# Two self-attention loops with a third probability buffer, another order on each engine, and evenly spread projection pieces

## The chip, the cores and the metric

The kernel runs on one core of a Trainium2 chip. The metric is device time in microseconds, the median of three runs. A core has TensorE (matmuls, with a separate queue of weight loads), VectorE, ScalarE, GpSimd, and SyncE, which here issues most of the transfers. Each engine executes its own instructions in order, and engines wait for each other through semaphores.

## What is computed

Two transformer blocks on 512 tokens of width 1024, in float32. The first block (dilated attention, convolutional feed-forward) isn't touched. The second block computes three attentions from one projection, gates and merges them, and then runs a mixture of 16 experts. Cut to the two attentions concerned:

```
h = rmsnorm(x);  proj = h @ w_in
# differential attention: 8 heads, two maps m each, head size 64, value size 128
sc = q[m] . k[m] * scale - slope[head] * |qpos - kpos|      # 512 x 512
p  = softmax(sc);  a = p[0] - lam * p[1];  o = a @ v
# window attention: 16 heads of 64, 4 key heads, window of 128 to each side
sc = q . k * scale - slope[head] * dist, or -inf outside the window
p  = softmax(concat(sc, sink))[:-1];  o = p @ v
```

## The kernel before

The sequence has 4 query blocks of 128 rows. The first changed loop, here DA, is differential attention: 16 units u (and two more rounds to drain), a unit being one head (u // 2) and half of the query blocks (u % 2), so four score tiles of 128 x 512 (two query blocks, two maps). The second, WA, is window attention: 16 units of one pair of heads and two query blocks, four score tiles of 128 x 256 or 128 x 384. All is written out by hand, engine by engine; the order in each queue is the order of the code.

One round u of DA, before:
- TensorE: four score matmuls of unit u into four PSUM banks (L1507); the product with V of unit u-2 (L1516); eight transposes of the probabilities of unit u-1 (L1526); then the fill of this round.
- VectorE: the probabilities of unit u-1 (`da_probs`: reciprocal L1049, L1051, then for each of two query blocks a scaling L1054 and a multiply-add L1055); then for unit u four times "add the distances, write to `da_e`, take the maximum" (L1071) and the negated maximum (L1076).
- ScalarE: the PSUM eviction of a finished fill job (L697, L701); the output of a head (L710); two copies of transposed probabilities of u-1 (L717); four exponentials of u, in place, with row sums (L722).
- GpSimd: it splits the projection weights of the fill into a high and a low part (L457, L460), two instructions for each job of 128 output features, as soon as the buffers of the job two before are free; between these it makes the distance tables of later heads (L505; for WA L509, in pairs), released by the maxima that last used them.

`da_e`, `da_pt`, `mx`, `nmx`, `lsum` have two copies each, used by u % 2. Because of that the maxima of unit u wait until the transposes of u-2 have been done.

Round u of WA is alike: scores (L1542), product with V of u-2 (L1558), then eight transposes of u-1 in two groups (L1567), two k of fill, a third group of two transposes, which needs the PSUM bank that ScalarE has emptied by its first copy, then the rest of the fill. ScalarE copies all three groups (L742) and then does the exponentials of u (L755, and L757 for the sink). VectorE does probabilities of u-1 (L1085, L1086, L1090), then maxima (L1105, L1110) of u.

The fill (`FILL1`, `FILL2`, `proj_part`) is the projection of later inputs: 10 jobs of 8 k in DA and 8 jobs of 8 k in WA, where one k is three matmuls of 128 x 512 (L1486 to L1488; high x high, high x low, low x high). All jobs use PSUM bank 3, so each waits for ScalarE's eviction of the one before. In DA the even jobs lie whole in round 3c, the odd ones in two halves in rounds 3c+1 and 3c+2; in WA each job has four k in each of two rounds.

Of the kernel before, what the change touches and what calls it, by code (L numbers as in the profile page):

```python
# [15 lines left out]
S, D, P = 512, 1024, 128  # L16
TT, KT = S // P, D // P
# [28 lines left out]
def build(nc, I, out):  # L46
# [3 lines left out]
    with ctx:  # L50
# [99 lines left out]
        da_e = ar(4096, 2, 4, S)  # L150
        da_pt = ar(8192, 2, 4, 256)
        wdist = ar(11776, 384)
        dist = ar(12160, 896)
        alibi = ar(13056, 2, 896)
        walibi = ar(13312, 4, 384)
        lamv = ar(8192, 4, 64)
        wa_q, wa_k, wa_v = ar(0, KT, S), ar(27136, WA_KV, S), ar(29184, TT, 256)
        o_wa = wa_q
        wa_p = ar(4096, 2, 4, 384)
        wa_pt = ar(8192, 20, P)  # L160
        memt = ar(23040, 2, D)
        memn = ar(25088, 2, D)
        junkm = ar(12160, D)
# [92 lines left out]
        FILL1 = [[] for _ in range(18)]  # L256
        FILL2 = [[] for _ in range(18)]
        for j in range(10):
            if j % 2 == 0:
                FILL1[3 * (j // 2)] = [(j, range(8))]  # L260
            else:
                FILL1[3 * (j // 2) + 1] = [(j, range(4))]
                FILL1[3 * (j // 2) + 2] = [(j, range(4, 8))]
        for j in range(8):
            FILL2[2 * j] = [(j, range(4))]
            FILL2[2 * j + 1] = [(j, range(4, 8))]

        def fill_ended(fill, u):

            return [j for j, ks in fill[u] if ks[-1] == KT - 1] if u >= 0 else []  # L270
# [161 lines left out]
        def _(pool):  # L432
# [85 lines left out]
            wtmp = ar(30208, 384)  # L518
# [45 lines left out]
        def _(act):  # L564
# [139 lines left out]
            for u in range(18):  # L704
                for j in fill_ended(FILL1, u - 1):
                    wa_feature(j)
                if u >= 3 and u % 2:
                    h = (u - 3) // 2
                    act.wait_ge(dpv, u - 1)
                    A(o_raw[:, h, :], ps[:, 2, :], F.Copy).then_inc(dO_ev, 1)  # L710
# [8 lines left out]
                if u < 16:  # L719
                    act.wait_ge(dnm_done, u + 1)  # L720
                    for i in range(4):
                        last = A(da_e[:, u % 2, i, :], da_e[:, u % 2, i, :], F.Exp, bias=nmx[:, u % 2, i:i + 1],  # L722
                                 accum_out=lsum[:, u % 2, i:i + 1])
                    last.then_inc(de_done, 1)
            act.dma_start(memt, I["mem_2"][0].rearrange("(t p) d -> p t d", p=P)).then_inc(in_mem, 16)

            act.wait_ge(in_small, 96)
            for u in range(18):
                for j in fill_ended(FILL2, u - 1):
                    act.wait_ge(pj_ps, J_F2 + j + 1)  # L730
                    A(xa_q[:, j, :], ps[:, 3, :], F.Copy, scale=0.0625).then_inc(pjA, 1)
                if u >= 3 and u % 2:
                    act.wait_ge(wpv, u - 1)
                    A(o_wa[:, (u - 3) // 2, :], ps[:, 2, :], F.Copy).then_inc(wO_ev, 1)
                if 1 <= u <= 16:
                    m = u - 1
                    for i, nb in enumerate((4, 4, 2)):
                        act.wait_ge(wt_ps, 3 * m + i + 1)
                        if m >= 2:
                            act.wait_ge(wpv, m - 1)  # L740
                        b0 = 10 * (m % 2) + 4 * i
                        A(wa_pt[:, b0:b0 + nb, :], ps[:, i % 2, 0:nb * P].rearrange("p (b q) -> p b q", b=nb),  # L742
                          F.Copy).then_inc(wpt_done, 1)
# [5 lines left out]
                if u < 16:  # L749
                    act.wait_ge(wnm_done, u + 1)  # L750
                    p, qh = u // 2, u % 2
                    for i in range(4):
                        c0, c1 = (P if (qh, i // 2) == (0, 0) else 0), (256 if (qh, i // 2) == (1, 1) else 384)
                        v = wa_p[:, u % 2, i, c0:c1]
# [5 lines left out]
                    last.then_inc(we_done, 1)  # L760

# [93 lines left out]
        def _(dve):  # L855
# [190 lines left out]
            def da_probs(u):  # L1046
# [5 lines left out]
                for i in range(2):  # L1052
                    e0, e1 = da_e[:, u % 2, 2 * i, :], da_e[:, u % 2, 2 * i + 1, :]
# [5 lines left out]
            for u in range(17):  # L1059
                if u:  # L1060
                    da_probs(u - 1)
                if u < 16:
# [3 lines left out]
                    if u >= 2:  # L1066
                        dve.wait_ge(dt_ps, 2 * (u - 1))
                    for i in range(4):
                        qb = 2 * (u % 2) + i // 2
                        dve.wait_ge(sd_ps, 4 * u + i + 1)  # L1070
                        V.tensor_tensor_reduce(out=da_e[:, u % 2, i, :], in0=ps[:, 4 + i, :],  # L1071
# [21 lines left out]
            for u in range(17):  # L1093
                if u:
                    wa_probs(u - 1)
# [690 lines left out]
```

## Time and profile before

| | |
|---|---|
| median of three runs | 2738.1 us (2730.5 to 2738.1) |
| profiled execution | 2739.4 us, span 2737.6 us |
| TensorE matmul busy | 2386.6 us (87%) |
| VectorE, ScalarE, GpSimd busy | 948.2, 497.2, 1024.2 us |
| mean granted TensorE clock | 0.959 of full speed |

The trace times are counted from the span's start. TensorE's matmuls are pipelined, so two of them overlap in the rows; the time of a sequence is read from start to start. "Idle before" is the idle time of the engine ahead of an instruction, with what ended it. A granted clock of 1 is 2.4 GHz, one of 0.5 is 1.2 GHz, and a value between them is a mean over time.

### The profile page before, as it was taken

To read this page: it belongs to the slowest core of one execution; us is meant where nothing else is said; L and a number is where in the kernel's file an instruction comes from. 1 tells how busy PE (TensorE), PEld (TensorE's weight loads), DVE (VectorE), ACT (ScalarE), POOL (GpSimd) and SP (SyncE) were. 2 spreads that over 40 slices of the span, in tenths; PEclk is the share of its full clock that TensorE was granted. 3 is DMA by queue.
4 is the path that set the end of the run, shared out by engine and by line. 5 is a ranking of instruction groups with operands and counts; after the bars stand their busy time and mean duration, and the time that the engine had idled before them with its cause. 6 is when DMAs were issued, how large, how long until landed. Compare 5 with 4: busy or idle time off the path is not lost.

```text
span 2737.6 us, 27015 instructions
## 1 busy us (share of the span) xinstructions
PE 2386.6 (87%) x11244; PEld 1581.4 (58%) x11244; DVE 948.2 (35%) x1323; ACT 497.2 (18%) x1067; POOL 1024.2 (37%) x497
## 2 busy tenths in 40 slices
PE   6999968999989988787899999599888888888886
PEld 4778837887878856565668887533323232332322
DVE  4664664555020156544732363401111101021012
ACT  2324222121010044454431010100000000000001
POOL 5444606888787744332538887200000000000000
PEclk9999989999999999898999999699999999999999
DMA  4211202322222210100213224489999999999996
GB/s 133 70 47 47 93 0 66 104 93 92 93 93 79 93 47 31 47 32 31 93 53 101 93 93 154 184 363 416 416 418 417 418 417 417 416 416 417 417 418 279
DMA packets 172341, 527.43 MB, mean 193 GB/s; under 512 B 9954, under 2 KB 92091, under 8 KB 139451
## 3 DMA queue, kind: packets, MB, share of 16 engines
q1 hardware_dynamic: 169008, 521.17, 49.1%
q10 hardware_dynamic: 3211, 4.51, 0.5%
q8 instruction: 90, 1.47, 0.2%
q14 instruction: 32, 0.26, 0.0%
HBM read 523.56 MB, written 2.10 MB: 192 GB/s over the span
## 4 chain that ended last, share of the span: by engine, by line
PE 67%; DMA 13%; DVE 12%; ACT 5%; issue 2%; ACTq 0%; POOL 0%; SPq 0%; DVEq 0%; POOLq 0%
PE ps L1298 9%; PE ps L1299 9%; PE ps L1300 9%; PE ps L1756 8%; PE ps L1729 7%; DMA hT<-in_w_exp_up 5%; PE ps L1451 4%; DMA arena<-in_w_exp_up 4%; DMA ring<-in_w_exp_up 4%; PE ps L1314 3%; PE ps L1315 2%; PE ps L1316 2%; PE ps L1690 2%; ACT arena L722 1%; PE ps L1714 1%
## 5 line engine op out<-in xcount | busy, mean ns | idle before, releaser
L457 POOL TENSOR_TENSOR w_hi<-ring,one 128x1024 fp32r<-128x1024 f32 x208 | 403.8, 1942 | 516.4 <-PE ps L1300 285.7
L460 POOL TENSOR_TENSOR w_lo<-ring,w_hi 128x1024 fp32r<-128x1024 f32 x222 | 543.4, 2448 | 58.0 <-ACT w_hi L773 41.6
L1298 PE MATMUL ps<-h_hi,w_hi 128*128 128x512 f32 x864 | 346.2, 401 | 8.4 <-DVE h_lo L880 5.8
L1300 PE MATMUL ps<-h_hi,w_lo 128*128 128x512 f32 x864 | 337.7, 391 | 0.0
L1299 PE MATMUL ps<-h_lo,w_hi 128*128 128x512 f32 x864 | 337.7, 391 | 0.0
L552 POOL TENSOR_TENSOR arena<-arena 128x512 f32<-128x512 f32 x8 | 8.4, 1048 | 834.6 <-PE ps L1702 796.8
L1729 PE MATMUL ps<-ring,arena 128*64 128x512 f32 x944 | 212.6, 595 | 42.6 <-DMA ring<-in_w_exp_up 41.8
L1729 PE MATMUL ps<-arena 128*64 128x512 f32 x848 | 191.9, 595 | 39.8 <-DMA arena<-in_w_exp_up 39.8
L1298 PEld LDWEIGHTS ps<-h_hi,w_hi 128*128 128x128 f32 x864 | 163.1, 189 | 50.4 <-DVE h_lo L880 6.7
L1299 PEld LDWEIGHTS ps<-h_lo,w_hi 128*128 128x128 f32 x864 | 163.2, 189 | 36.8 <-issue 4.3
L1300 PEld LDWEIGHTS ps<-h_hi,w_lo 128*128 128x128 f32 x864 | 162.9, 189 | 34.6
L1729 PEld LDWEIGHTS ps<-ring,arena 128*64 128x64 f32 x944 | 71.5, 137 | 180.5 <-issue 179.4
L1729 PEld LDWEIGHTS ps<-arena 128*64 128x64 f32 x848 | 64.6, 137 | 164.2 <-issue 164.0
L1234 DVE TENSOR_TENSOR arena<-ps,arena 64x1024 f32<-64x1024 f32 x32 | 39.3, 1227 | 306.1 <-ACT arena L834 305.4
L834 ACT ACTIVATE arena<-ps 64x1024 f32<-64x1024 f32 x32 | 30.8, 1009 | 571.0 <-PE ps L1729 571.0
L1756 PE MATMUL ps<-arena 128*64 128x512 f32 x528 | 123.4, 615 | 11.7 <-DVE arena L1265 11.7
L1243 DVE TENSOR_TENSOR x<-ps,x 128x512 f32<-128x512 f32 x64 | 42.9, 689 | 260.3 <-PE ps L1714 259.9
L908 DVE RECIPROCAL arena<-arena 128x512 f32<-128x512 f32 x24 | 80.5, 3353 | 68.9 <-ACT arena L629 68.8
L1009 DVE SCALAR_TENSOR_TENSOR arena<-ps,vec,arena 128x511 f32<-128x511 f32 (+1 forms) x88 | 59.9, 743 | 110.9 <-ACT arena L668 110.9
L1756 PE MATMUL ps<-ring,arena 128*64 128x512 f32 x416 | 92.2, 593 | 5.5 <-DVE arena L1265 5.5
L1272 DVE COPY arena<-ps 64x512 f32<-64x512 f32 x16 | 11.1, 694 | 225.5 <-PE ps L1756 225.5
L1756 PEld LDWEIGHTS ps<-arena 128*64 128x64 f32 x528 | 38.0, 141 | 87.1 <-issue 72.7
(297 smaller groups left out, 3903.4 us busy)
## 6 DMA issues: line engine op xcount, KB each, us to landing
arena<-in_w_exp_down SPq DMA_DIRECT2D x66, 1024.0 KB, 19.9
ring<-in_w_exp_gate SPq DMA_DIRECT2D x59, 1024.0 KB, 24.1
ring<-in_w_exp_up SPq DMA_DIRECT2D x59, 1024.0 KB, 25.4
arena<-in_w_exp_gate SPq DMA_DIRECT2D x53, 1024.0 KB, 21.8
arena<-in_w_exp_up SPq DMA_DIRECT2D x53, 1024.0 KB, 23.0
ring<-in_w_exp_down SPq DMA_DIRECT2D x52, 1024.0 KB, 22.0
ring<-in_w_in SPq DMA_DIRECT2D x34, 1024.0 KB, 5.1
ring<-in_ffn_w_up SPq DMA_DIRECT2D x22, 1024.0 KB, 5.1
```

Of the source, the lines that this page charges most:

```text
L457: nc.gpsimd.tensor_tensor(hi, w, one[:].unsqueeze(2).to_broadcast(list(w.shape)), ALU.mult).then_inc(w_high, 1)
L460: nc.gpsimd.tensor_tensor(lo, w, hi.bitcast(f32), ALU.subtract).then_inc(w_split, 1)
L908: V.reciprocal(rr[:, n % 2, :], rt[:, n % 2, :]).then_inc(rr_done, 1)
L1009: V.scalar_tensor_tensor(out=v, in0=ps[:, 2 * (j % 2) + i, 0:S - sh], scalar=vec[:, CW + 44 * k + 22 * i + j:CW + 44 * k + 22 * i + j + 1] ...
L1298: mm(o, w[0][:, k, :], h[0][:, k, 0:ntok], start=(k == 0), stop=False)
L1299: mm(o, w[0][:, k, :], h[1][:, k, 0:ntok], start=False, stop=False)
L1300: last = mm(o, w[1][:, k, :], h[0][:, k, 0:ntok], start=False, stop=(k == KT - 1))
L1314: mm(o, hi, w[0][:, k - k0, :], start=(k == 0), stop=False)
L1315: mm(o, hi, w[1][:, k - k0, :], start=False, stop=False)
L1451: last = mm(ps[:, 2 * t + half, :], tile_of(a_, f, t), w_[:, 0, half * 512:half * 512 + 512], start=(f == 0 and a_ is act_hi and w_ is w[0 ...
L1729: last = mm(ps[64 * i:64 * i + 64, c, :], xeT[:, k, a * CAP:(a + 1) * CAP], w[:, c * 512:c * 512 + 512], start=(k == 0), stop=(k == KT - 1))
L1756: last = mm(ps[64 * half:64 * half + 64, 4, :], act_e[:, f, :], w[:, j * D + half * 512:j * D + half * 512 + 512], start=(f == 0), stop=(f ...
```

## The change

- `da_e` and `wa_p` get a third copy (u % 3). `da_pt`, `wa_pt`, the distance tables and scratch areas move to other places of the arena.
- VectorE does the maxima of unit u before the probabilities of u-1, in both loops. The maxima wait for the transposes of u-3 instead of u-2; the negated maximum waits also for the exponentials of u-2.
- ScalarE does the exponentials of u before the head's output and the copies of u-1. In WA the third copy of u-2 comes ahead of the exponentials of u, the first two copies of u-1 behind them.
- TensorE: each round's fill has two parts, one ahead of the product with V, one behind it and ahead of the transposes, which are last in the round. In DA two jobs are spread over three rounds as 3+3, 2+3, 2+3 k; in WA each round has 2+2. In WA the third group of transposes moves to the next round, right behind its scores.
- ScalarE evicts a job that ended in a second part at the start of the next round, one that ended in a first part in the same round ahead of the exponentials.

```diff
-        da_e = ar(4096, 2, 4, S)
-        da_pt = ar(8192, 2, 4, 256)
+        da_e = ar(4096, 3, 4, S)
+        da_pt = ar(10240, 2, 4, 256)
...
-        wa_p = ar(4096, 2, 4, 384)
-        wa_pt = ar(8192, 20, P)
+        wa_p = ar(4096, 3, 4, 384)
+        wa_pt = ar(8704, 20, P)
...
+        for c in range(5):
+            j = 2 * c
+            FILL1[3 * c] = ((j, range(3)), (j, range(3, 6)))
+            FILL1[3 * c + 1] = ((j, range(6, 8)), (j + 1, range(3)))
+            FILL1[3 * c + 2] = ((j + 1, range(3, 5)), (j + 1, range(5, 8)))
         for j in range(8):
-            FILL2[2 * j] = [(j, range(4))]
-            FILL2[2 * j + 1] = [(j, range(4, 8))]
+            FILL2[2 * j] = ((j, range(2)), (j, range(2, 4)))
+            FILL2[2 * j + 1] = ((j, range(4, 6)), (j, range(6, 8)))
...
             for u in range(18):
-                for j in fill_ended(FILL1, u - 1):
+                for j in fill_ended(FILL1, u - 1, 1) + fill_ended(FILL1, u, 0):
                     wa_feature(j)
+                if u < 16:
+                    act.wait_ge(dnm_done, u + 1)
+                    for i in range(4):
+                        last = A(da_e[:, u % 3, i, :], da_e[:, u % 3, i, :], F.Exp, bias=nmx[:, u % 2, i:i + 1],
+                                 accum_out=lsum[:, u % 2, i:i + 1])
+                    last.then_inc(de_done, 1)
                 if u >= 3 and u % 2:
...
             for u in range(17):
-                if u:
-                    da_probs(u - 1)
                 if u < 16:
...
-                    if u >= 2:
-                        dve.wait_ge(dt_ps, 2 * (u - 1))
+                    if u >= 3:
+                        dve.wait_ge(dt_ps, 2 * (u - 2))
...
+                    if u >= 2:
+                        dve.wait_ge(de_done, u - 1)
                     V.tensor_scalar(nmx[:, u % 2, :], mx[:, u % 2, :], -1.0, None, ALU.mult).then_inc(dnm_done, 1)
+                if u:
+                    da_probs(u - 1)
...
+                if FILL1[u][0]:
+                    proj_part(J_F1 + FILL1[u][0][0], FILL1[u][0][1])
                 if u >= 2:
...
                     last.then_inc(dpv, 1)
+                if FILL1[u][1]:
+                    proj_part(J_F1 + FILL1[u][1][0], FILL1[u][1][1])
                 if 1 <= u <= 16:
...
+                if u >= 2:
+                    pe.wait_ge(wpt_done, 3 * (u - 2) + 1)
+                    wa_T(u - 2, 2)
+                if FILL2[u][0]:
+                    proj_part(J_F2 + FILL2[u][0][0], FILL2[u][0][1])
...
-                if 1 <= u <= 16:
-                    pe.wait_ge(wpt_done, 3 * m + 1)
-                    wa_T(m, 2)
-                for j, ks in FILL2[u]:
-                    proj_part(J_F2 + j, ks[2:])
```

## Rows read from the trace of the kernel before

**Rows 1.** Windows: us, busy (count) of PE, PEld, DVE, ACT, POOL; clock; DMA; GB/s.

```profile
965.70:1142.00 176.30, 143.22 (x628) 99.64 (x630) 113.74 (x243) 79.18 (x186) 71.14 (x37) 0.91 0.11 36
1142.00:1299.00 157.00, 122.65 (x800) 92.52 (x796) 72.42 (x240) 75.40 (x228) 47.86 (x28) 0.87 0.11 34
```

**Rows 2.** Chain of waits, 960 to 1300, shares by line.

```profile
by line: ACT arena L722 10.8%; ACT arena L755 10.2%; issue 9.8%; PE ps L1567 8.3%; DVE arena L1071 7.3%; DVE arena L1054 7.2%; DVE arena L1090 5.6%; PE ps L1486 4.5%; DVE arena L1055 4.5%; PE ps L1487 4.4%; PE ps L1488 4.3%; PE ps L1516 2.8
```

**Rows 3.** Waits, 965 to 1130: us in total, times, longest.

```profile
DVE rl L1049 <- ACT arena L722: 49.4, 16, 3.7
...
PE ps L1526 <- DVE arena L1055: 22.8, 9, 5.1
```

**Rows 4.** Waits, 1130 to 1295, same columns.

```profile
DVE lsum L1085 <- ACT esink L757: 76.8, 16, 7.2
...
PE ps L1567 <- DVE arena L1090: 33.7, 16, 4.3
```

**Rows 5.** Timeline of VectorE, one DA unit: start, us, engine, line, operation, [idle before].

```profile
1062.75 0.68 DVE L1071 CUSTOM_DVE_ANT_0 arena<-ps,arena 128x512 f32<-128x512 f32 x1
...
1065.31 0.17 DVE L1076 TENSOR_SCALAR nmx<-mx 128x4 f32<-128x4 f32 x1
...
1068.48 0.18 DVE L1049 RECIPROCAL rl<-lsum 128x4 f32<-128x4 f32 x1 [3.00 <-ACT arena L722]
...
1070.67 0.75 DVE L1055 SCALAR_TENSOR_TENSOR arena<-arena,rl 128x512 f32<-128x512 f32 x1
```

**Rows 6.** Timeline of all engines, 1000 to 1022: GpSimd and VectorE.

```profile
1003.02 2.45 POOL L505 TENSOR_SCALAR arena<-arena 128x896 f32<-128x896 f32 x1 [4.79 <-DVE mx L1071]
...
1007.27 2.38 POOL L457 TENSOR_TENSOR w_hi<-ring,one 128x1024 fp32r<-128x1024 f32 x1 [1.79 <-PE ps L1488]
...
1007.81 2.12 DVE L1054 TENSOR_SCALAR arena<-arena,rl 128x512 f32<-128x512 f32 x1
...
1009.97 2.71 DVE L1055 SCALAR_TENSOR_TENSOR arena<-arena,rl 128x512 f32<-128x512 f32 x1
```

**Rows 7.** Timeline of all engines, 1186 to 1209 (WA).

```profile
1186.93 1.09 PE L1567 MATMUL ps<-ident,arena 128*128 128x128 f32 x8 [0.41 <-DVE arena L1090]
...
1193.35 3.22 DVE L1090 TENSOR_SCALAR arena<-arena,rl 128x384 f32<-128x384 f32 x4
...
1201.25 0.50 ACT L755 ACTIVATE arena<-arena,nmx 128x256 f32<-128x256 f32 x1
...
1202.26 1.35 PE L1542 MATMUL ps<-arena 64*128 64x384 f32 x8
...
1203.54 1.31 PE L1558 MATMUL ps<-arena 128*64 128x128 f32 x20
...
1203.93 0.16 DVE L1085 TENSOR_TENSOR lsum<-lsum,esink 128x4 f32<-128x4 f32 x1 [5.53 <-ACT esink L757]
...
1205.67 1.09 PE L1567 MATMUL ps<-ident,arena 128*128 128x128 f32 x8 [0.82 <-DVE arena L1090]
...
1208.00 0.38 PE L1567 MATMUL ps<-ident,arena 128*128 128x128 f32 x2
```

**Rows 8.** Timeline of all engines, 1000 to 1022: TensorE.

```profile
1001.95 0.40 PE L1488 MATMUL ps<-h_hi,w_lo 128*128 128x512 f32 x1
...
1006.73 0.39 PE L1488 MATMUL ps<-h_hi,w_lo 128*128 128x512 f32 x1
...
1007.05 1.99 PE L1507 MATMUL ps<-arena 64*128 64x512 f32 x8
...
1008.96 1.99 PE L1516 MATMUL ps<-arena 128*128 128x256 f32 x8
...
1012.74 1.09 PE L1526 MATMUL ps<-ident,arena 128*128 128x128 f32 x8 [1.78 <-DVE arena L1055]
```

**Rows 9.** Timeline of TensorE at the end of DA.

```profile
1134.88 1.97 PE L1526 MATMUL ps<-ident,arena 128*128 128x128 f32 x8 [8.80 <-DVE arena L1055]
```

**Rows 10.** Instructions of L1071 over the span: ns min/median/max, first and last start.

```profile
L1071 DVE CUSTOM_DVE_ANT_0 arena<-ps,arena x64: 677/685/692, 969.7 to 1123.9; 128x512 f32<-128x512 f32 x64
```

More of the change, by code:

```diff
@@ L254, in pj_bank_free, with fill_ended @@
                 eng.wait_ge(pjA if PJ[m] == "A" else pjD, PJ[:m + 1].count(PJ[m]))
[L256 to L263, printed above, removed]
-        for j in range(8):
-            FILL2[2 * j] = [(j, range(4))]
-            FILL2[2 * j + 1] = [(j, range(4, 8))]
-        def fill_ended(fill, u):
-            return [j for j, ks in fill[u] if ks[-1] == KT - 1] if u >= 0 else []
+        FILL1 = [((), ()) for _ in range(18)]
+        FILL2 = [((), ()) for _ in range(18)]
+        for c in range(5):
[3 more added lines that the diff above has]
+            FILL1[3 * c + 2] = ((j + 1, range(3, 5)), (j + 1, range(5, 8)))
+        for j in range(8):
+            FILL2[2 * j] = ((j, range(2)), (j, range(2, 4)))
+            FILL2[2 * j + 1] = ((j, range(4, 6)), (j, range(6, 8)))
+        def fill_ended(fill, u, part):
+            job = fill[u][part] if u >= 0 else ()
+            return [job[0]] if job and job[1][-1] == KT - 1 else []
         def pj_all_done(eng, n):
@@ L760, in _ @@
                     last.then_inc(we_done, 1)
+                if u >= 3 and u % 2:
+                    act.wait_ge(wpv, u - 1)
+                    A(o_wa[:, (u - 3) // 2, :], ps[:, 2, :], F.Copy).then_inc(wO_ev, 1)
+                if 1 <= u <= 16:
+                    wa_copy(u - 1, 0)
+                    wa_copy(u - 1, 1)
             act.wait_ge(n_sq, nbase[3] + 2)
@@ L1093, in _ @@
             for u in range(17):
-                if u:
-                    wa_probs(u - 1)
                 if u < 16:
@@ L1113, in _ @@
                                            op0=ALU.mult, op1=ALU.min).then_inc(wnm_done, 1)
+                if u:
+                    wa_probs(u - 1)
             norm(3, memt, memn)
@@ L1525, in _ @@
                         for kb in range(4):
-                            last = nc.tensor.transpose(ps[:, i, kb * P:(kb + 1) * P], da_e[:, m % 2, 2 * i, kb * P:(kb + 1) * P], ident[:])
+                            last = nc.tensor.transpose(ps[:, i, kb * P:(kb + 1) * P], da_e[:, m % 3, 2 * i, kb * P:(kb + 1) * P], ident[:])
                         last.then_inc(dt_ps, 1)
-                for j, ks in FILL1[u]:
-                    proj_part(J_F1 + j, ks)
             pe.wait_ge(sd_done, 64)
@@ L1543, in _, with wa_T @@
                            start=True, stop=True).then_inc(sw_ps, 1)
+                def wa_T(m, i):
+                    for j, (b, qb, kb) in enumerate(WA_UNIT[m % 2][4 * i:4 * i + 4]):
+                        c = (kb - qb + 1) * P
+                        last = nc.tensor.transpose(ps[:, i % 2, j * P:(j + 1) * P], wa_p[:, m % 3, b, c:c + P], ident[:])
+                    last.then_inc(wt_ps, 1)
+                if u >= 2:
+                    pe.wait_ge(wpt_done, 3 * (u - 2) + 1)
+                    wa_T(u - 2, 2)
+                if FILL2[u][0]:
+                    proj_part(J_F2 + FILL2[u][0][0], FILL2[u][0][1])
                 if u >= 2:
@@ L1561, in _ @@
                     last.then_inc(wpv, 1)
-                def wa_T(m, i):
-                    for j, (b, qb, kb) in enumerate(WA_UNIT[m % 2][4 * i:4 * i + 4]):
-                        c = (kb - qb + 1) * P
-                        last = nc.tensor.transpose(ps[:, i % 2, j * P:(j + 1) * P], wa_p[:, m % 2, b, c:c + P], ident[:])
-                    last.then_inc(wt_ps, 1)
+                if FILL2[u][1]:
+                    proj_part(J_F2 + FILL2[u][1][0], FILL2[u][1][1])
                 m = u - 1
```

57 lines of the change are left out of this document (24 added, 33 removed).

## Prediction

> **What bounds the kernel now.** After the page I took the busy time of the two stretches that the change touches. The first loop (differential attention, "DA") fills 965.7 to 1142, 176.3 us; TensorE is busy 143.2 of them, at a mean granted clock of 0.91. The second (window attention, "WA") fills 1142 to 1299, 157.0 us; TensorE is busy 122.7, at 0.87. VectorE is busy 114 and 72 us, ScalarE 79 and 75 [rows 1]. So no engine is full, and TensorE falls now and then from 2.4 to 1.2 GHz.
>
> The chain of waits over both loops says why: it runs over the exponentials (L722, L755), the VectorE lines (L1071, L1054, L1090, L1055) and the transposes (L1567), and the fill matmuls (L1486 to L1488) have only about 4.5% each [rows 2]. The waits agree. In DA VectorE waits 49.4 us for the exponentials (16 times), and TensorE idles 22.8 us ahead of the transposes until L1055 is done [rows 3]. In WA it is 76.8 us (16 times) and 33.7 us [rows 4].
>
> One unit without disturbance shows the ring. In DA: scores added and maximum taken 1062.75 to 1065.31 (2.56), then the exponentials until the reciprocal at 1068.48 (3.17), then the probabilities until 1070.67 + 0.67 (2.86). Sum 8.6 us [rows 5]; 16 units are 137 us. The next unit's maxima come after the probabilities, in the same VectorE queue, and its exponentials after the maxima, so VectorE and ScalarE take turns. The other 39 us are head, tail and collisions: at 1007.81 a scaling takes 2.12 us, and at 1009.97 a multiply-add 2.71; undisturbed these are 0.75 us for the multiply-add and about 0.5 for the scaling (1068.48 to 1070.67 is 2.19 for the reciprocal and L1051, some 0.2 each, two scalings and one multiply-add), each while GpSimd works [rows 5, 6]. In WA the ring is longer: transposes at 1186.93 and 1205.67 are two units apart, 9.4 us each [rows 7], 150 us in 16 units. There ScalarE's third copy, which waits for transposes behind two pieces of fill (1208.00, 2.33 us after the first), lies ahead of the exponentials in ScalarE's queue.
>
> **What the change makes of the ring.** VectorE does maxima(u) before probabilities(u-1), ScalarE does exponentials(u) before the copies of u-1, and the third buffer lets maxima(u) be written while the transposes of u-1 have not read theirs. So exponentials(u-1) run beside maxima(u), and the 3.17 us (DA) and 2.7 us (WA, 1201.25 to 1203.93) [rows 5, 7] leave the ring. Nothing is computed more or less; no DMA moves except the memory load at the end of ScalarE's first loop, which still comes after it. The wait for the exponentials of u-2 ahead of the negated maximum costs nothing: they are a whole unit old. What is late next is TensorE's own queue.
>
> **DA, TensorE work.** Scores 1007.05 to 1008.96: 1.91. The product with V is as long by its row (1.99 with the last one's end, 1.91 by the spacing), transposes 1.09. One k of fill is three matmuls; seven k from 1001.95 to 1006.73 are 0.683 each, 80 k are 54.6 us [rows 8]. 16 x (1.91 + 1.91 + 1.09) + 54.6 = 133.2 us at full clock. One unit with five k is 8.3, with six 9.0.
>
> **DA, where TensorE waits.** Take the time from a unit's first score matmul. Maxima end at 3.2, the negation at 3.4, probabilities at 3.4 + 2.9 = 6.3. The transposes stand in TensorE's queue behind scores, V product and fill, at 7.2 (five k) or 7.9 (six). So an undisturbed unit has 0.9 to 1.6 us of slack, and VectorE is hidden. Disturbed ones are not, and the new order puts the disturbances on the probabilities:
> - A fill job that ends in the first part of a unit (3c+1: units 4, 7, 10, 13) ends at 1.91 + 1.37 = 3.3. That releases GpSimd's two splits, 1.9 and 2.4 us (1007.27 and after: the first began right as its job ended) [rows 6, 8]. The two together cost the probabilities (2.12 - 0.5) + (2.71 - 0.75) = 3.6 us there, so I take 3.7: ready at 10.0, 2.8 late. 4 x 2.8 = 11.2.
> - A slope (2.45 us, released by the last maximum of an odd unit: 1003.02, where now it runs beside the exponentials) [rows 6] falls on the probabilities of units 3, 5, 9, 11: some 2.0 each, ready at 8.4, late by 0.6, 1.2, 0.6 and, with the mask instructions behind it, about 2.7. Sum 5.1. In the other odd units the splits delay the slope past the probabilities.
> - Jobs that end in a second part release splits at about 7.2, and these are over by 3.3 of the next unit. Nothing.
> - Head: VectorE starts 4 us late as now, probabilities(0) meet splits: 4.9. Tail: units 15 to 17 have no fill, and four WA slopes and a split meet the last two probabilities. Now the transposes wait 8.80 us there and run at half clock, 1.97 instead of 1.09 [rows 9, 8]. I take 6.5 for unit 14's, three waits of 0.8 for copies, and 3 for the clock: 11.9.
> - Clock dips elsewhere after a stall: 2.
> Sum: 133.2 + 11.2 + 5.1 + 4.9 + 11.9 + 2 = 168.3, against 176.3: **8 us less**. The bounds: if no collision delays TensorE in the middle and the tail costs half, 133 + 5 + 6 + 2 = 146. If all of GpSimd's 71.1 us in this stretch [rows 1] fell on the ring of scores, maxima, negation, probabilities, transposes (0.6 + 2.6 + 0.2 + 2.9 + 1.1 = 7.4 a unit), 16 x 7.4 + 71 = 189. I stay at 168, since the release times put about half of the splits and slopes there.
>
> The Trainium skill (SBUF — State Buffer, Who interferes with whom) says that VectorE instructions in a two-port mode, or with two SBUF inputs against a GpSimd instruction that reads SBUF, share one port pair with GpSimd under an exclusive lock, and that whoever issues first blocks the other for the whole instruction. That speaks against this order, which places the port-using probabilities right where slopes and splits are released; the durations of 2.12 and 2.71 us agree. The maxima, which read PSUM and SBUF, never grow: 0.677 to 0.692 us in all 64 [rows 10]. By the rule alone and every time lost to it, the result is the third rival below.
>
> **WA, TensorE work.** Scores 1202.26 to 1203.54: 1.28 to 1.35 (1.3), V product 1.3, eight transposes 1.09, two more 0.38 (1208.00) [rows 7], four k of fill 2.73 [rows 8]. 6.85 a unit, 109.6 in all. **Where it waits.** Maxima and negation end at 2.5, probabilities take about 1.8 (VectorE starts at 1203.93 and releases the transposes at 1205.67) [rows 7], ready at 4.3. The transposes are due at 1.35 + 0.38 + 1.37 + 1.3 + 1.37 = 5.8: slack 1.5. Exponentials(u) run 2.6 to 5.3, and the copies of u-1 start at 6.4, so ScalarE (75.4 / 16 = 4.7 of 6.85 us) [rows 1] is hidden too; the third copy now needs transposes that stand right behind the scores, 1.7, before the exponentials can start at 2.6. Jobs end in odd units at 5.8, so their splits are over by 3.2 of the next, even, unit: no cost. Slopes come in pairs, 2.4 us from 2.2 in odd units: ready at about 6.1, 0.4 late, 6 to 8 times, 3 us. In the trace of before a pair of splits makes 3.22 us of the four scalings, about 1.9 too much [rows 7], and that delay I no longer see on the path. Head 2, tail 2.7 (copies that nothing covers), clock 3: TensorE would be 95% busy where it is now 78%, so most of the dips (0.87 mean is 41 us at half clock, 2 x 0.13 x 157) should go. Sum 109.6 + 3 + 2 + 2.7 + 3 = 120.3 against 157.0: **37 us less**. Bounds: 115 with no collision and no dip; with all 47.9 us of GpSimd [rows 1] on a ring of 0.4 + 2.1 + 1.8 + 1.1 + 0.3 = 5.7 a unit, 139.
>
> **After the loops** nothing changes: the memory projection, the gates and the experts start from TensorE's and ScalarE's progress, and SyncE's first expert transfers wait for the gates, so all of it moves earlier by the same amount. The moved buffers (masks, distances, copies) cost nothing by themselves.
>
> **The number.** The profiled execution took 2739.4 us (span 2737.6), 1.3 over the median of the runs, 2738.1. 8.0 + 36.7 = 44.7 less: 2694.7 from the one, 2693.4 from the other. I say 2694.
>
> **Rivals.**
> 1. TensorE-bound: collisions fall beside slack. 146 + 115 = 261 against 333, 72 less: 2666. For it: all slack above is positive without collisions, and the clock rises. Against: the release times of splits in units 4, 7, 10, 13.
> 2. Collisions cost VectorE more than reckoned: halfway between my sum and the upper bounds (189 + 139 = 328): 308, 25 less, 2713. For it: the nine double or single hits could be fourteen. Against: WA's splits lie clear of the probabilities.
> 3. VectorE replaces the ring: every GpSimd instruction hits, 328 us, 5 less, 2733. Within 0.3%. Against: splits released at 7.2 fall on maxima, which don't grow.
> 4. Slower: as 3, and TensorE, waiting 2 to 3 us in each of the 32 units, stays at 1.2 GHz for the scores, copies' wait and V product that follow. Transposes behind a long wait take 0.9 us more [rows 9]; with the V product (1.9 more) 1 to 3 us a unit. With 2 it is 64 us: 328 + 64 - 333 = 59 more, 2797; slower by over 0.3% from 0.4 us a unit on. Against: now waits of 22.8 us in nine leave the mean clock at 0.91 [rows 1, 3].
> 5. It doesn't do what it says: an engine's new order waits for itself, e.g. ScalarE's fill copy ahead of exponentials(u) waits for a job that ends at 3.3, when the maxima are ready at 3.4. Priced 0.5 us in 5 units: nothing against the rest.
>
> **How the numbers follow.** About 0.3% (8 us) can be told from no change. Forecast (2680 to 2706): 0.60. Rival 1 (2660 to 2680): 0.18. Rival 2 (2706 to 2730): 0.15. Rival 3, same: 0.04. Rival 4: 0.03. Range 2664 to 2718. Faster 0.93, same 0.04, slower 0.03.
>
> **What would show it.** In the profile after: VectorE's wait for the exponentials falls from 49 and 77 us to below 10 each; TensorE above 90% busy in WA, with a clock over 0.95, and unit spacing of 6.9 us; in DA spacing of 8.3 to 9 with stretches of 11 in every third unit, where L1054 and L1055 take over 2 us beside L457 and L460. Wrong it would be if the transposes wait in most units of WA, if the slopes' collisions show in even units too, or if a later stage gives the time back by waiting for weights.

## The result, and the profile after

The changed kernel takes 2685.7 us in the median (2681.1 to 2690.9, four runs) against 2734.9 for the kernel before; the ratio is 0.982 [0.980, 0.983]. 2694 was forecast, in a range of 2664 to 2718. Its profiled execution (the slowest of the four) has a span of 2689.1 us, 48.5 less than before. In its code the lines have moved: scores L1516 (DA) and L1553 (WA), maxima L1074 and L1110, negation L1081 and L1117, L1056 for the old L1051, scaling L1059, multiply-add L1060, transposes L1539 and L1560, V product L1527 and L1582, exponentials L710 and L754, fill L1495 to L1497.

The page's span and its slices of the granted clock, then the two loops from first score matmul to first score matmul, and to the end of WA (columns as in [rows 1]):

```profile
span 2689.1 us, 27043 instructions
...
PEclk9999979999999999999999999699999999999999
```

```profile
963.50:1132.80 169.30, 143.45 (x624) 98.22 (x624) 115.43 (x243) 78.62 (x185) 71.64 (x37) 0.93 0.11 34
1132.80:1247.00 114.20, 108.90 (x801) 79.25 (x800) 70.74 (x240) 76.57 (x230) 49.34 (x28) 1.00 0.16 53
```

Between the same marks the loops of before took 175.5 and 157.5 us (965.7 to 1141.2 to 1298.7, inside the windows of [rows 1]). The last mark of before is the end of the last V product; after the change that is at 1246.3, and the row above runs 0.7 us past it. Like for like, DA gained 6.2 us and WA 44.0 (157.5 to 113.5), together 50.2. What stands ahead of the loops is 2.2 us shorter. What stands behind them is 3.9 longer (1442.8 against 1438.9). Of this, 1.7 lies in the memory projection right behind WA: its first to its last matmul take 30.4 us (1255.4 to 1285.8) against 28.7 (1307.8 to 1336.5), and the granted clock of the 20 us behind WA is 0.74 against 0.82. The rest I leave open. In WA TensorE is now busy 108.9 of 113.5 us at the upper level, 2.4 GHz: 14.5 us of the gain is the same matmuls at a higher clock (mean 0.87 before, 1.00 now), 29.5 is idle time gone. In DA it is still idle for 25.9 us, and the clock is 0.93.

The waits in DA (963 to 1131), then in WA (1131 to 1242); us in total, times, longest:

```profile
ACT arena L710 <- DVE nmx L1081: 44.8, 15, 5.3
DVE arena L1074 <- PE ps L1516: 42.3, 16, 4.2
...
PE ps L1539 <- DVE arena L1060: 23.0, 7, 5.0
```

```profile
DVE arena L1110 <- PE ps L1553: 43.5, 16, 8.0
...
DVE lsum L1092 <- ACT esink L756: 1.1, 1, 1.1
...
PE ps L1560 <- DVE arena L1097: 1.3, 1, 1.3
```

VectorE's wait for the exponentials, 49.4 and 76.8 us before [rows 3, 4], is gone in DA and 1.1 us in WA. In its place VectorE waits for TensorE's scores, 16 times in each loop: TensorE leads. TensorE's own wait for the probabilities fell in WA from 33.7 us in 16 waits [rows 4] to 2.8 in two: the 1.3 listed, and one of 1.5 at 1242.77, behind the end of the listed window. In DA it is 23.0 in 7 waits. Before, it was 22.8 in 9 [rows 3] and the 8.80 at 1134.88 [rows 9], which stands behind the end of that window, so 31.6. Of the 8.6 us that went, 5.5 are in the tail (8.80 became 3.30, at 1122.59). The rest of the loop waits nearly as much as before, but in other places. The transposes that waited (timeline of TensorE, start, us, [idle before]) are, among others, those of units 0, 3, 6 and 9, in rounds 1, 4, 7 and 10:

```profile
981.26 1.97 PE L1539 MATMUL ps<-ident,arena 128*128 128x128 f32 x8 [5.00 <-DVE arena L1060]
...
1012.33 1.09 PE L1539 MATMUL ps<-ident,arena 128*128 128x128 f32 x8 [3.28 <-DVE arena L1060]
...
1043.78 1.54 PE L1539 MATMUL ps<-ident,arena 128*128 128x128 f32 x8 [4.38 <-DVE arena L1060]
...
1074.13 1.20 PE L1539 MATMUL ps<-ident,arena 128*128 128x128 f32 x8 [3.28 <-DVE arena L1060]
```

Those that did not wait have no bracket: 991.86, 1000.70, 1022.20, 1031.08. One round with a collision, all engines (VectorE and GpSimd of round 7):

```profile
1033.31 0.69 DVE L1074 CUSTOM_DVE_ANT_0 arena<-ps,arena 128x512 f32<-128x512 f32 x1 [3.27 <-PE ps L1516]
...
1035.76 1.89 POOL L457 TENSOR_TENSOR w_hi<-ring,one 128x1024 fp32r<-128x1024 f32 x1 [8.95 <-PE ps L1497]
1035.88 1.80 DVE L1081 TENSOR_SCALAR nmx<-mx 128x4 f32<-128x4 f32 x1
...
1037.73 2.39 POOL L460 TENSOR_TENSOR w_lo<-ring,w_hi 128x1024 fp32r<-128x1024 f32 x1
1037.80 2.35 DVE L1056 TENSOR_SCALAR rl<-rl,lamsc 128x2 f32<-128x2 f32 x1
...
1040.19 1.23 DVE L1059 TENSOR_SCALAR arena<-arena,rl 128x512 f32<-128x512 f32 x1
1040.21 2.45 POOL L505 TENSOR_SCALAR arena<-arena 128x896 f32<-128x896 f32 x1
...
1042.12 0.81 DVE L1059 TENSOR_SCALAR arena<-arena,rl 128x512 f32<-128x512 f32 x1
```

The fill job ends, both splits are released, and two instructions of VectorE on 4 and on 2 elements a row take 1.80 and 2.35 us; undisturbed they are 0.17 and 0.23. In this round a slope (L505) follows the splits, and the two scalings beside it take 1.23 and 0.81 us instead of 0.49: 1.1 us in all, by which the wait here (4.38) exceeds the 3.28 of rounds 4 and 10. From here on there were two questions: which of the parts made the gain, and whether these collisions are what DA still loses.

### The profile page after: what moved, and what is told of

Read it like the earlier page. It is cut to its first block, busy times and chain, and to the rows that moved or that the text cites. A ratio compares the mean times of both kernels' runs of the same rounds, so it can differ in the third digit from the quotient of the medians.

```text
span 2689.1 us, 27043 instructions
## 1 busy us (share of the span) xinstructions
PE 2372.0 (88%) x11244; PEld 1567.0 (58%) x11244; DVE 948.9 (35%) x1323; ACT 497.4 (18%) x1067; POOL 1024.7 (38%) x497
## 4 chain that ended last, share of the span: by engine, by line
PE 71%; DMA 13%; DVE 11%; ACT 2%; issue 2%; ACTq 0%; POOL 0%; SPq 0%; DVEq 0%; POOLq 0%
PE ps L1307 9%; PE ps L1308 9%; PE ps L1309 9%; PE ps L1767 8%; PE ps L1740 7%; DMA hT<-in_w_exp_up 5%; PE ps L1460 5%; DMA arena<-in_w_exp_up 4%; DMA ring<-in_w_exp_up 4%; PE ps L1323 3%; PE ps L1325 3%; PE ps L1324 3%; PE ps L1701 2%; PE ps L1725 1%; PE ps L1516 1%
## 5 line engine op out<-in xcount | busy, mean ns | idle before, releaser
L1307 PEld LDWEIGHTS ps<-h_hi,w_hi 128*128 128x128 f32 x864 | 162.6, 188 | 50.2 <-DVE h_lo L885 6.7
## 6 DMA issues: line engine op xcount, KB each, us to landing
arena<-in_w_exp_up SPq DMA_DIRECT2D x53, 1024.0 KB, 23.3
```

What stands on the lines that cost most here:

```text
L1307: mm(o, w[0][:, k, :], h[0][:, k, 0:ntok], start=(k == 0), stop=False)
```

## The experiments

"DA" and "WA" below are the times from the first score matmul of DA to the first of WA, and from there to the last score matmul, each from the run's one trace. Before they are 175.5 and 140.2, after the change 169.4 and 99.8.

| run | median us | ratio to before | DA | WA |
|---|---|---|---|---|
| e1 WA alone | 2692.9 | 0.984 [0.983, 0.986] | 175.6 | 100.0 |
| e2 VectorE's old order | 2708.2 | 0.990 [0.988, 0.991] | 175.3 | 116.5 |
| e3 ScalarE's old order | 2727.2 | 0.997 [0.996, 0.998] | 184.5 | 125.1 |
| e4 two copies | 2690.8 | 0.984 [0.982, 0.985] | 170.7 | 103.3 |
| e5 fill in its old place | 2795.9 | 1.022 [1.020, 1.023] | 221.1 | 156.0 |
| e6 jobs end late | 2676.6 | 0.978 [0.977, 0.980] | 156.0 | 99.7 |
| e7 GpSimd waits | 2662.0 | 0.973 [0.971, 0.974] | 146.1 | 99.7 |
| e8 e3 with earlier eviction | 2709.5 | 0.990 [0.989, 0.992] | 176.9 | 110.3 |
| e9 e6 and e7 | 2667.7 | 0.976 [0.974, 0.977] | 152.7 | 99.7 |
| e10 only DA's splits wait | 2660.4 | 0.973 [0.972, 0.974] | 142.7 | 99.8 |
| e11 before, splits wait | 2719.3 | 0.995 [0.994, 0.997] | 169.5 | 129.9 |
| e12 e2, splits wait | 2703.2 | 0.989 [0.987, 0.991] | 167.0 | 115.0 |

The window loop of e11 is coded as before; its 129.9 against 140.2 is discussed there.

### Which part made the gain

**e1.** DA's orders and fill as before, WA as changed.

> Window loop as in the changed kernel, differential loop as in the kernel before (orders, fill and two-copy rule of the waits; the third buffer is only storage). My theory: the two loops' gains are separate; the window loop gave 157.5 - 114.1 = 43 us in the traces and the differential loop 175.5 - 169.4 = 6 us, so this one is 43 us below before, 2692 us, ratio 0.984. Rival: the window loop only gains because the first loop hands over earlier (probability split still under way at the border): then 10 us or more less gain, 2702 us.

As expected, 2692.9: the gains are separate, and WA has most of it.

**e2.** VectorE's old order in both loops:

```diff
             for u in range(17):
+                if u:
+                    da_probs(u - 1)
                 if u < 16:
...
-                if u:
-                    da_probs(u - 1)
```

> The changed kernel with VectorE's old order in both loops (probabilities of u-1 ahead of the maxima of u). My theory: the ring of maxima, exponentials and probabilities returns in the differential loop (8.6 us a unit plus collisions, about 175 us, 6 more than changed). In the window loop the same ring is only 2.1 + 2.7 + 1.8 = 6.6 us a unit, about TensorE's 6.8, plus some collisions: 120 to 130 us, 6 to 16 more. Together 2698 to 2708 us. Rival A (VectorE's order is the whole gain): about 2735 us. Rival B (it does nothing): 2686 us.

2708.2, with 175.3 us in DA and 116.5 in WA. The waits of DA (960 to 1140; L1083 is the negated maximum, L1054 the reciprocal) show the ring again:

```profile
ACT arena L710 <- DVE nmx L1083: 83.8, 16, 8.8
DVE rl L1054 <- ACT arena L710: 48.0, 16, 3.0
```

VectorE waits for the exponentials 16 times for 3 us, ScalarE for the maxima. And in WA VectorE's order makes only 17 of the 40 us by which the time between first and last score matmul fell. The old WA was not bound by this ring alone.

**e3.** ScalarE's old order in both loops: copies of u-1 and the head's output ahead of the exponentials of u.

> The changed kernel with ScalarE's old order in both loops (head's output and copies of u-1 ahead of the exponentials of u). My theory: the exponentials of u then begin at about 9.1 in the differential loop and end at 3.9 of the next unit, just inside VectorE's slack of 0.9 us, so only the units with collisions lose, 0.6 us each; in the window loop they end at 3.4 of the next unit, probabilities at 5.3, transposes due at 5.8. 0 to 8 us more than changed: 2686 to 2694 us. Rival (both orders are needed to open the ring): 2715 us or more.

2727.2, 33 us above the end of my expectation: a miss. It is only 0.3% faster than the kernel before, and DA, at 184.5, is slower than before the change. That the exponentials come late is not what costs: TensorE's wait for the probabilities is 24.5 us in DA (23.0 as changed) and 1.3 in WA (2.8). Three rows of the waits, the first of DA (963 to 1131), the others of WA (1131 to 1290):

```profile
PE ps L1495 <- ACT arena L697: 9.1, 5, 2.1
```

```profile
PE ps L1495 <- ACT arena L740: 14.8, 7, 2.1
...
PE ps L1582 <- ACT arena L734: 7.4, 9, 3.3
```

TensorE waits for ScalarE: fill matmuls (L1495) for the eviction of the PSUM bank that all fill jobs share (L697, L740), and the V product for the third copy (L734). Both stand in ScalarE's queue behind a block of four exponentials. One such place in the timeline (1198 to 1204 and the rows ahead of it):

```profile
1197.12 0.58 ACT L740 ACTIVATE arena<-ps 128x512 f32<-128x512 f32 x1
...
1197.75 0.79 PE L1495 MATMUL ps<-h_hi,w_hi 128*128 128x512 f32 x1 [2.11 <-ACT arena L740]
```

The matmuls behind this wait take 0.79 and then 0.63 us; the same places of a later k take 0.50 and 0.39 (1201.98). The granted clock is 0.50, the lower level of 1.2 GHz, from 1197.75 to 1200.50, after 1.00 from 1190 to 1195.

**e8** tests this reading: ScalarE's order stays old, but the bank is evicted in the round in which its job ends, ahead of the copies.

```diff
-                for j in fill_ended(FILL1, u - 1, 1) + fill_ended(FILL1, u, 0):
+                for j in fill_ended(FILL1, u, 0) + fill_ended(FILL1, u, 1):
                     wa_feature(j)
...
+                if 2 <= u:
+                    wa_copy(u - 2, 2)
-                for j in fill_ended(FILL2, u - 1, 1):
+                for j in fill_ended(FILL2, u, 1):
```

> As the kernel with ScalarE's old order (2727 us), but a fill job's PSUM bank is evicted in the round in which the job ends, ahead of the copies and so ahead of the exponentials, not behind them. My theory: the old order cost 41 us because TensorE's next fill waits for that bank behind the exponentials (9.1 us in 5 waits in the differential loop, 14.8 us in 7 in the window loop) and the clock falls after it; this gives 24 to 30 us of it back, about 2700 us; the third copy, still behind the exponentials, keeps the rest. Rival (the exponentials themselves come too late for the probabilities): 2720 us or more.

2709.5: 18 of the 41 us come back, less than the 24 to 30 expected. 7.6 us are in DA, 14.8 in WA. So the bank is the larger single cause in WA. For the rest e8's own trace shows where TensorE loses it. In DA 7.5 us remain against the changed kernel: its wait for the probabilities is 26.2 us (23.0), it is busy 147.0 us (143.5) with the same matmuls at a granted clock of 0.91 (0.93), and it waits 0.8 more for copies. So a part of this does come from later probabilities. In WA 10.5 us remain, and there the V product waits 9.8 us in 13 waits for ScalarE's copies, of which the third is still behind the exponentials; as changed it doesn't wait there before the last scores. The wait for the probabilities is 1.3. No run moved the third copy by itself.

**e4.** Two copies of the probabilities, the maxima of u waiting for the transposes of u-2.

```diff
-                    if u >= 3:
-                        dve.wait_ge(dt_ps, 2 * (u - 2))
+                    if u >= 2:
+                        dve.wait_ge(dt_ps, 2 * (u - 1))
...
-                        V.tensor_tensor_reduce(out=da_e[:, u % 3, i, :], in0=ps[:, 4 + i, :],
+                        V.tensor_tensor_reduce(out=da_e[:, u % 2, i, :], in0=ps[:, 4 + i, :],
```

> The changed kernel with two copies of the probabilities instead of three (maxima of u wait for the transposes of u-2). My theory: TensorE's queue has the transposes of u-2 ahead of the scores of u in the differential loop, so the third copy does nothing there; in the window loop two of the ten transposes stand behind the scores, and maxima start 1.3 us later, within a slack of 1.5. 0 to 5 us more than changed, 2686 to 2691. Rival (the third copy carries the change, as its name says): the loops fall back toward the old spacing, 2700 us or more.

2690.8, 5 us above the changed kernel with intervals that overlap. The third copy of the probabilities, first in the name of the change, is worth 0 to 5 us. In DA it can do nothing: TensorE's queue has the transposes of u-2 in round u-1, ahead of the scores of u, without which there are no maxima. In WA two of ten transposes stand behind the scores; there 3.5 us are lost.

**e5.** Orders and copies as changed, the fill behind the transposes as before.

```diff
-            FILL1[3 * c] = ((j, range(3)), (j, range(3, 6)))
-            FILL1[3 * c + 1] = ((j, range(6, 8)), (j + 1, range(3)))
-            FILL1[3 * c + 2] = ((j + 1, range(3, 5)), (j + 1, range(5, 8)))
+            FILL1[3 * c] = ((), (j, range(8)))
+            FILL1[3 * c + 1] = ((), (j + 1, range(4)))
+            FILL1[3 * c + 2] = ((), (j + 1, range(4, 8)))
```

> The changed kernel (both orders, three copies) with the fill of each round as before: whole behind the transposes, 8, 4 and 4 k in the differential loop, 4 k in each round of the window loop. My theory: the transposes of u-1 then stand only 3.8 us (2.7 in the window loop) behind the first score matmul and wait until the probabilities are ready at 6.3 (4.3); the fill then comes on top: 6.3 + 1.1 + 3.4 = 10.8 us a unit in the differential loop (it had 9.9), 4.3 + 1.1 + 2.7 = 8.1 in the window loop (6.8 as changed). 10 to 18 and 20 us more than changed: 2716 to 2726 us, most of the gain lost. Rival (the new orders alone carry the gain, spreading the fill only smooths): 2690 us or less.

2795.9, 110 us above the changed kernel and 61 above the one before. The direction was expected, the size was far off. The waits in DA, the windows of both loops, and a round of DA:

```profile
PE ps L1537 <- DVE arena L1060: 52.5, 14, 6.1
```

```profile
961.00:1182.00 221.00, 163.76 (x626) 115.30 (x624) 98.12 (x243) 79.74 (x186) 71.03 (x37) 0.82 0.08 26
1182.00:1340.00 158.00, 116.15 (x726) 85.87 (x728) 70.44 (x230) 70.64 (x211) 44.73 (x26) 0.88 0.10 32
```

```profile
1000.66 1.97 PE L1537 MATMUL ps<-ident,arena 128*128 128x128 f32 x8 [4.23 <-DVE arena L1060]
...
1008.69 1.99 PE L1516 MATMUL ps<-arena 64*128 64x512 f32 x8
...
1009.99 0.69 DVE L1074 CUSTOM_DVE_ANT_0 arena<-ps,arena 128x512 f32<-128x512 f32 x1 [9.38 <-PE ps L1516]
```

L1537 are its transposes. With nothing between V product and transposes, TensorE waits 3.8 us on average in each of 14 rounds. In WA it waits 36.4 us for the probabilities in 15 waits (2.8 as changed), and the granted clock is 0.88 there too. The same matmuls are busy 20.3 us longer than in the changed kernel (163.8 against 143.5), at a clock of 0.82, and VectorE starts its maxima 1.3 us after the first score matmul, not 0.6 as I had reckoned. The kernel before, with the fill in this same place, had 31.6 us of these waits in DA; my reading, not tested by itself, is that its probabilities came first in VectorE's queue. So the new orders of VectorE and ScalarE are only good with the fill ahead of the transposes; with the old place they are worse than nothing. No run has VectorE's new order alone.

### What DA still lost

**e6.** DA's jobs end right ahead of the transposes, none in the first part of a round:

```diff
-            FILL1[3 * c] = ((j, range(3)), (j, range(3, 6)))
-            FILL1[3 * c + 1] = ((j, range(6, 8)), (j + 1, range(3)))
-            FILL1[3 * c + 2] = ((j + 1, range(3, 5)), (j + 1, range(5, 8)))
+            FILL1[3 * c] = ((j, range(1)), (j, range(1, 4)))
+            FILL1[3 * c + 1] = ((j, range(4, 5)), (j, range(5, 8)))
+            FILL1[3 * c + 2] = ((j + 1, range(4)), (j + 1, range(4, 8)))
```

> The changed kernel with the differential loop's fill as 1+3, 1+3 and 4+4 k, so that every job ends right ahead of the transposes and none releases GpSimd's two splits at 3.3 us, when the probabilities begin. My theory: the waits for the transposes in units 4, 7, 10 and 13 (about 2.7 us each) go and little comes for them: 8 to 12 us less than changed, 2674 to 2678 us. Rival (the waits come from VectorE's own length, not from the collision; shorter fill ahead of the transposes makes them longer): 2686 us or more.

2676.6, as expected: 9 us less, 13.4 in DA.

**e7.** The fill as changed; GpSimd waits for the probabilities of the round.

```diff
                     c, view, _, _ = halves[i]
+                    r = i - stage["f1"] - 2
+                    if r >= 0 and r % 2 == 0 and r < 10:
+                        pool.wait_ge(a_done, 3 * (r // 2) + 1)
+                    if r == 9:
+                        pool.wait_ge(a_done, 16)
+                    if i == stage["mem"] + 1:
+                        pool.wait_ge(aw_done, 16)
...
                 pool.wait_ge(sd_done, 8 * (h - 1))
+                pool.wait_ge(a_done, 2 * h - 3)
                 slope(h)
```

> The changed kernel, in which GpSimd waits for the probabilities of the unit (a_done, in the last round of the window loop aw_done) before a split or a slope of the differential loop that would begin beside them; fill as changed. The four slopes for the window loop are left where they are. My theory: all collisions inside the differential loop go, and one of 3.7 us at the end of the window loop: 12 to 18 us less than changed, 2668 to 2674 us. Rival (VectorE's instructions are long for another reason, such as a late PSUM bank): 2686 us. Rival (GpSimd is then too late with the splits, and TensorE waits for them): 2690 us or more.

2662.0, 24 us less than the changed kernel and more than expected. DA, 964.6 to 1110.7, and WA, 1110.7 to 1225; then TensorE's wait in DA (L1547 are the transposes, L1068 the multiply-adds):

```profile
964.60:1110.70 146.10, 135.82 (x626) 94.99 (x626) 95.98 (x243) 77.72 (x185) 71.85 (x37) 0.98 0.11 37
1110.70:1225.00 114.30, 108.74 (x801) 79.19 (x800) 67.22 (x241) 78.37 (x232) 49.33 (x28) 1.00 0.16 54
```

```profile
PE ps L1547 <- DVE arena L1068: 7.4, 4, 3.3
```

TensorE's wait for the probabilities fell from 23.0 to 7.4 us, its busy time by 7.6 us as the clock rose from 0.93 to 0.98, and VectorE's busy time by 19.5 with the same instructions. That the collisions cost DA 23 us is shown: only the start of GpSimd's work is moved, and they go. Of the 23.3 us, 15.6 are the wait and 7.6 the clock after it; I had expected the wait alone.

**e10.** As e7, but only the splits of DA wait; the slopes' wait and the one at the end of WA are left out.

> As the kernel in which GpSimd waits (2662 us), but only the splits of the differential loop wait for the probabilities; the slopes start when the maxima are done, as in the changed kernel, and the wait at the end of the window loop is left out. My theory: the changed kernel's trace shows a slope beside the probabilities at a cost of 0.5 us (L1056 0.72 instead of 0.23 at 996.9), not of 2.0 as predicted, so the slopes' waits are worth 0 to 2 us; the last split over the window loop's last probabilities costs 3.7. 2664 to 2669 us. Rival (a slope blocks as a split does): four to six slopes at 1 to 2 us more, 2672 or more.

2660.4, the lowest median of all, below my expectation, with an interval that overlaps e7's. The window of DA, and the timeline in which a split now starts when the last multiply-add is over:

```profile
961.80:1104.50 142.70, 134.40 (x624) 94.34 (x624) 94.80 (x243) 77.79 (x185) 71.77 (x37) 0.99 0.12 38
```

```profile
999.03 0.75 DVE L1065 SCALAR_TENSOR_TENSOR arena<-arena,rl 128x512 f32<-128x512 f32 x1
...
999.87 1.90 POOL L462 TENSOR_TENSOR w_hi<-ring,one 128x1024 fp32r<-128x1024 f32 x1 [9.46 <-DVE arena L1065]
```

DA needs 142.7 us for TensorE work of 133. The slopes' waits were worth nothing; in DA they cost a little, since e7's trace has two waits of the maxima for a late slope, 5.3 us in all, and e10's has none.

**e9.** The fill of e6 with the waits of e7.

> GpSimd's waits (2662 us) and the fill whose jobs end late (2677 us) together. My theory: both take away the same collisions, splits on the probabilities. Without collisions the spread of 6, 5 and 5 k is the better one, since with 4 k the transposes are due at 6.6 and the probabilities are ready at about 7.0: 0.3 us in ten units. 2662 to 2667 us. Rival (the two remove different costs and add up): 2652 us.

2667.7, slightly above the expectation and above e7: the two remove the same cost, and without collisions the even spread is the better one.

**e11.** The kernel before, in which DA's splits wait (`a_done`, 3c+1 or 3c+3); nothing else changed.

> The kernel before, in which the splits of the differential loop wait for the probabilities of their unit (a_done), so that they run beside maxima and exponentials; nothing else is changed. My theory: the old ring of 8.6 us a unit stays, but the collisions in it go: L1054, L1055, L1051 and L1076 were about 12.7, 4.0, 4.1 and 3.6 us too long in all, of which the two pairs of the tail stay: 14 to 20 us less than before, 2716 to 2722 us, a ratio of 0.993 to 0.995. Rival (in the old order the collisions hide behind other waits): 2736 us.

2719.3, in the expected range, 0.5% less than before, but by luck: 14 to 20 us were expected from DA, and DA fell by 6 only. The splits now lie on the negation instead. Groups of VectorE in DA (negation, then scaling; count, busy us, mean ns, idle before):

```profile
L1079 DVE TENSOR_SCALAR nmx<-mx 128x4 f32<-128x4 f32 x16 | 19.5, 1220 | 0.6
L1057 DVE TENSOR_SCALAR arena<-arena,rl 128x512 f32<-128x512 f32 x32 | 18.1, 567 | 0.6
```

The scalings went down from a mean of 0.88 us to 0.57, the negation up from 0.39 to 1.22 (undisturbed 0.17). WA fell by 10 us although its code is as before. Its trace says where: TensorE waits as long for the probabilities (34.9 us in 16 waits, 33.7 before), but is busy 111.9 us instead of 123.5 with the same 801 matmuls, at a mean granted clock of 0.95 instead of 0.87. Why the clock stays up there is open. Two of the six executions took 2728 and 2731 us at a mean clock of 0.961, the other four 2716 to 2720 at 0.966 to 0.969. That the ring of before has no free place of 4.3 us for a pair of splits, since the negation stands between the maxima and the exponentials, is my reading; only this one placement was tried.

**e12.** VectorE's old order (e2) with such waits for DA's splits.

> The changed kernel with VectorE's old order in both loops (2708 us: differential loop 175.3, window loop 116 to the last score matmuls' 99.8) and with the splits of the differential loop waiting for the probabilities (2660 us with VectorE's new order, its differential loop 142.7). My theory: without collisions the old order is bound by the ring of 8.6 us a unit, and the moved splits hit the negated maximum instead, as they did when only they were moved in the kernel before (169.5): 158 to 165 us, window loop as in the 2708 run, in all 2692 to 2700 us. So VectorE's order is worth 32 us or more once collisions are gone, not 22. Rival (the ring hardly counts once collisions are gone, 16 x 8.6 = 138 is TensorE's work too): differential loop 146, 2681 us or less.

2703.2, a little above the expectation; DA 167.0. VectorE's new order is worth 22 us as changed (2708.2 to 2685.7) and 43 with splits that wait (2703.2 to 2660.4). The two runs of the second pair don't wait alike: in e12 the splits of both jobs wait, as in e11, and the negation takes 1.11 us in the mean; in e10 only the even ones and the last do, and it takes 0.23. So 43 holds for these two placements; a better one for the old order was not looked for.

## Why the prediction was right, and where it was not

**What bounded the kernel.** Right. A ring of maxima, exponentials and probabilities in DA, and one that is longer by transposes and the third copy in WA. e2 gives DA back its 175.3 us. In WA ScalarE's order counts for more than VectorE's (125.1 against 116.5 us with the old one), mostly through the bank of the fill (e8).

**TensorE's work as the new bound.** Right. 6.85 us a unit were worked out for WA; scores follow each other at 6.76, and 96% busy and a clock of 1.00 are as forecast. In DA the lower bound without collisions was 146 us; e7 has 146.1, and e10 with 142.7 is below it.

**DA: 168.3 forecast, 169.3 measured, partly by errors that cancel.** The gain was forecast as 8.0, and 6.2 were measured. The head was 4.9, measured 5.0. The four double collisions were 11.2; their waits are 3.28, 4.38, 3.28 and 2.25, in all 13.2. They land on negation and L1056, not on the scalings, with nearly the same sum. Three terms were mis-sized; all waits together were taken as 30 us and are 25.9, the clock was taken as 5 and is 10:
- The slopes, 5.1 us. None of their rounds 3, 5, 9 and 11 shows a wait. (The seventh wait, 1.49 at 1094.49, is in round 12, where a split starts late behind the mask instructions.) A slope beside probabilities (GpSimd, then VectorE, from their own timelines):

```profile
996.71 2.45 POOL L505 TENSOR_SCALAR arena<-arena 128x896 f32<-128x896 f32 x1 [0.24 <-DVE mx L1074]
```

```profile
996.94 0.72 DVE L1056 TENSOR_SCALAR rl<-rl,lamsc 128x2 f32<-128x2 f32 x1
997.70 0.49 DVE L1059 TENSOR_SCALAR arena<-arena,rl 128x512 f32<-128x512 f32 x1
998.22 0.75 DVE L1060 SCALAR_TENSOR_TENSOR arena<-arena,rl 128x512 f32<-128x512 f32 x1
```

It cost 0.5 us, not 2.0, and the next two instructions ran at full speed while it went on. The dearest slopes, right behind the splits in rounds 1 and 7, cost 1.0 and 1.1. The step that failed is the transfer of a split's price to a slope; e10, whose slopes don't wait, agrees.
- The tail. 6.5 us were taken for the transposes of unit 14, and they wait 3.30 (1122.59). The copies' waits, taken as three of 0.8, are 0.69 and 0.74.
- The clock: 2 in the middle and 3 in the tail were taken; TensorE is busy 143.5 us, 10 more than its 133 of full-clock work. Besides, maxima begin 1.3 us after the first score matmul (1032.04 to 1033.31), not 0.6, so the slack was 0.2 to 0.9 us, not 0.9 to 1.6.

**WA: 120.3 forecast, 113.5 measured.** The 3 us for slopes and 3 for the clock did not come; head and tail were 4.7, and all idle time of TensorE is 4.6. The last two splits make the four scalings of the last unit 4.98 us long, but TensorE waits only 1.5 for them. By the traces WA gained 7.3 us more than forecast, DA 1.8 less, and the rest of the kernel 1.7 less, which is the 3.8 between 44.7 and 48.5. The median missed by 8.3: it fell by 49.3, 4.6 more than forecast, and most of the other 3.7 lies in the base: 2738.1 was taken, the median of three executions, and it is 2734.9 with a fourth.

**The third copy.** The prediction gave it a part: it "lets maxima(u) be written while the transposes of u-1 have not read theirs". That was wrong. Two copies give this as well, since maxima(u) overwrite those of u-2; e4 puts the third at 0 to 5 us.

**ScalarE "is hidden".** True of the changed order, but the reason was thin: busy time says nothing of what stands behind a block of exponentials. e3 lost 41 us, 18 of them through such an eviction (e8), and my expectation repeated the mistake.

**The collisions.** The argument from the Trainium skill (SBUF — State Buffer, Who interferes with whom), that port-using probabilities now lie where the splits are released, is borne out: 23 us in DA by e7. By that rule the engine that issues first blocks the other for its whole instruction. That agrees with the splits (VectorE's 1.80 and 2.35 us end with them) and not with the slope above; here the measurement decides. Rivals 1 to 4 did not come; rival 1, with its 146 us, is what e7 shows to be possible.

## What to carry to other kernels

When a ring of two engines is opened by taking the next unit's first step ahead of this unit's last, look in the same edit at what stands behind that step in each queue. Here, of the 49 us, 27 were left without VectorE's new order, 8 without ScalarE's, and without filler ahead of the dependent matmuls the kernel was 61 us slower than before. Count a further buffer only if no queue already orders its reader ahead of the next writer. And look at what each finished job releases on the engine that shares ports with the critical one: semaphore waits of GpSimd ahead of its splits, and nothing else, were worth half as much as the whole change (e10, 25 us), and TensorE waited for no split because of them.

## What was not expected of the hardware

- GpSimd's elementwise product or difference of two tiles (128x1024, 1.9 and 2.4 us) holds up a VectorE instruction of 4 elements until its end (0.17 to 1.80 us), while a GpSimd tile-by-constant product (128x896, 2.45 us) held up one by 0.5 us and then let two others of 128x512 through at full speed; where it followed the splits directly it lengthened two scalings, by 1.1 us together.
- Waits of 3 to 5 us in TensorE show in the clock of the next matmuls: behind the waits of 5.00 and 4.38 us the transposes take 1.97 and 1.54 us instead of 1.03 to 1.09, and the granted clock from 981.26 to 986 is 0.50. Behind the wait of 3.28 in round 4 it is 0.66 from 1012.33 to 1016, behind that of 2.25 in round 13 it stays 1.00; but in e3 a wait of 2.11 was followed by 0.50. So the length of a wait alone doesn't say what it costs. In e5, 52.5 us of such waits go with 20.3 us more of matmul time for the same matmuls.
